# A recurrent decoder step: where the states of the sample sequences are loaded, summed and stored in the first tile

## The chip, the cores and the metric

The kernel runs on one core of a Trainium2 chip. The metric is device time in microseconds from start to end of one execution. The kernel before took 1485.17 us, the median of 3 runs (1482.73 to 1488.17).

## The reference, cut to what matters

One layer of a decoder is applied to a new sequence of 1024 tokens (the prompt) and, with the same weights, to one new token of each of 8 running sequences (the sample). Three groups of heads read one input projection and keep a recurrent state: GLA (6 heads, 32x64), DeltaNet (6 heads, 64x64) and HGRN2 (4 heads, 64x64). Then come an output projection, a mixture of 32 experts and a final norm.

```python
y_prompt, gla_p, dn_p, conv_p, hg_p = _trunk(x_prompt, z_gla, z_dn, z_conv, z_hg, *weights)
y_sample, gla_s, dn_s, conv_s, hg_s = _trunk(x_sample, state_gla, state_dn, state_conv, state_hgrn, *weights)
```

For a sample sequence the recurrence is a single step, here for DeltaNet (the other two have no correction of v):

```
S = exp(g) * S                        # decay of the state, (64 keys x 64 values) for each head
v = beta * (v - sum over keys k[key] * S[key, :])
S = S + k v^T                         # the new state: an output of the kernel
o = sum over keys q[key] * S[key, :]  # the output of the head
```

The states of all 8 sequences are inputs (`state_gla`, `state_dn`, `state_hgrn`) and, after the step, outputs of the same size: 0.375, 0.75 and 0.5 MB.

## The kernel before, in words

The prompt is cut into 8 tiles of 128 tokens (t = 0 to 7). For each tile TensorE computes the input projection in 17 units, one for each chunk of columns of w_in (mostly 1 MB); then follow the chunked recurrences, the output projection and the router. Behind the last tile come the experts (from 1087 us), which read their weights from HBM.

The engines have their own instruction streams, written out by hand, and wait for each other by semaphores: `done(eng, name, t)` waits until step `name` of tile t is over, `freed` until the tile before has given a buffer back. Nothing is reordered; an instruction that waits holds everything behind it on its engine.

**Weights.** SP issues the loads of the chunks, in the order of `stream`, into a ring of 4 buffers. `load_chunk(n)` waits until chunk n - 4 has been used. Chunks 0 to 16 are those of tile 0 (there TensorE runs the unit of the prompt, L1517 and L1521, and then that of the sample, L1534, whose semaphore `s_unit` frees the buffer), 17 to 33 those of tile 1, which TensorE computes while it works on tile 0's recurrence.

**The sample step.** The 8 x 16 sample states lie in `state_s`, one (sequence, head) in each partition: 48 rows of DeltaNet (`R_DN`), 48 of GLA, 32 of HGRN2; 4096 columns, key-major. SP loads them (L514 to L516) between chunks 11 and 12, when GpSimd has zeroed the space (`s_zero`). The 8 rows of projected values go to HBM by ScalarE's queue and come back to this layout by 16 small loads of SP (L536). VectorE then does the step in body(0), spread between its work for the prompt: `decay_s` (L1343, L1344), `read_keys_s` (L1347, the product with k), `correct_s` (L1350, the sum over keys), `update_s` (L1355, L1356 and the product with q, L1358; the step `s_state` is over behind L1356), `read_s` (L1361, the sum over keys; step `s_use`). The products are written to `tmp_s`, which is the space of E, zq and zk; so ScalarE's first exponentials of tile 0 (`decays(0)`, L897) wait for `s_use`.

**What lies on the states.** `state_s` shares its columns with vn, oc, x2, s_lin and s_dn of the prompt. Before these may be written the new states have to be in HBM. GpSimd stores them in body(0) behind its products for all four groups (L676 to L678), waits for the three stores, zeroes s_lin and s_dn (L680, L681; step `s_reset`), and goes on with the convolution of tile 1 (L590 to L604). ScalarE waits for `s_stored` in `load_x2` (L962), where it fetches the residual input into x2. That call stands in the loop over the levels, ahead of `norm_x(2)` (L754 to L760) and of the copy of level 5's product (L908), which TensorE needs for its next matmuls (L1479).

Of the kernel before, what the change touches and what calls it, by code (L numbers as in the profile page):

```python
# [6 lines left out]
ALU = mybir.AluOpType  # L7
ACT = mybir.ActivationFunctionType
AX = mybir.AxisListType.X
# [3 lines left out]
P = 128  # L13
# [66 lines left out]
NU = len(CHUNKS)  # L80
# [146 lines left out]
def trunk(nc, ctx, A, O, arena_cols, take, psum, bank, const, masks, x2_d, h2_d, lg, rows_d, so_d):  # L227
# [78 lines left out]
    st1, st2, st_s, gate_s, so, ng_s = take(4), take(4), take(4), take(64), take(64), take(64)  # L306
# [11 lines left out]
    def region(first, last):  # L318
        a, b = first.offset % 53200, last.offset % 53200 + last.shape[-1]
        return arena_cols(a, b)  # L320
# [17 lines left out]
    R_DN, R_GLA, R_HG = slice(0, 48), slice(48, 96), slice(96, 128)  # L338
# [7 lines left out]
    state_s = region(vn, s_spare)  # L346
    vec, ks_s = qs[:, 0:258], qs[0:48, 322:386]
# [14 lines left out]
    def step(name):  # L362
        name = once[name][0] if name in once else name
        if name not in sems:
            sems[name] = ctx.semaphore(name)
        return sems[name]

    def done(eng, name, t, n=1, per=1):

        eng.wait_ge(step(name), (once[name][1] if name in once else t * per) + n)  # L370
# [5 lines left out]
    def unit_at(t, k):  # L376

        return t * NU + (LAST_ORDER.index(k) if t == NT - 1 else k)
# [33 lines left out]
    n = 0  # L412
# [29 lines left out]
    def k_of(dt, rows=slice(0, P)):  # L442
        return qk2[rows, 4 + dt, :]
# [11 lines left out]
    with nc.Block() as block:  # L455
        @block.sync
        def _(sp):
            pb = lambda ap, n=P: ap.partition_broadcast(n)

            def load_chunk(n):  # L460
                kind, t, k = stream[n]
                if n >= RING:
                    was, wt, wk = stream[n - RING]
                    if was == "out":
                        sp.wait_ge(step("s_wo"), wk + 1) if wt == NT - 2 else sp.wait_ge(step("wo"), 4 * wt + wk + 1)
                    elif wt == 0:
                        sp.wait_ge(step("s_unit"), wk + 1)
                    else:
                        sp.wait_ge(step("unit_done"), unit_at(wt, wk) + 1)
                if kind == "in":  # L470
                    w, width = CHUNKS[k]
                    src = win_v[:, :, w:w + width]
                else:
                    width = WIDE
                    src = wout_v[:, :, WIDE * k:WIDE * k + WIDE]
                sp.dma_start(ring[n % RING][:, :, 0:width], src).then_inc(step(f"w_in{n % RING}"), 16)
# [32 lines left out]
            sp.dma_start(masks, A["shape_masks"]).then_inc(step("consts_in"), 16)  # L509
            for n in range(7, 12):  # L510
                load_chunk(n)
            sp.wait_ge(step("s_zero"), 2)
            sd_in = step("s_states_in")
            sp.dma_start(state_s[R_HG, :], A["state_hgrn"][0].rearrange("b h k e -> (b h) (k e)")).then_inc(sd_in, 16)  # L514
            sp.dma_start(state_s[R_GLA, 0:2048], A["state_gla"][0].rearrange("b h k e -> (b h) (k e)")).then_inc(sd_in, 16)
            sp.dma_start(state_s[R_DN, :], A["state_dn"][0].rearrange("b h k e -> (b h) (k e)")).then_inc(sd_in, 16)  # L516
            for n in range(12, NU + 5):
                load_chunk(n)


# [3 lines left out]
            q, k, dec, v_, o = 0, 64, 128, 192, ROW_AT  # L524
# [12 lines left out]
            sp.dma_start(O[8][0, :, 0:2, :], A["state_conv"][0, :, 1:3, :]).then_inc(st, 16)  # L537
            for n in range(NU + 5, NU + NU):
                load_chunk(n)
            done(sp, "s_out", 0)  # L540
            for n, (ap, h) in enumerate(((so[R_GLA, :], 6), (so[R_DN, :], 6), (so[R_HG, :], 4))):
                sp.dma_start(so_d[:, 384 * n:384 * n + 64 * h].rearrange("b (h e) -> b h e", e=DV), ap).then_inc(step("o_out"), 16)
# [32 lines left out]
        def _(pool):  # L575
# [34 lines left out]
            def body(t):  # L610
                n = t + 1
# [43 lines left out]
                for dt in range(4):  # L655
                    R = slice(0, DT_ROWS[dt])
# [4 lines left out]
                    e, k = E[dt % 2][R, :], k_of(dt, R)  # L661
# [9 lines left out]
                        ins = g.tensor_copy(el[R, dt:dt + 1], e[:, 1023:1024])  # L671
                    ins.then_inc(step("zks"), 1)
                if not t:
                    done(pool, "s_state", 0)
                    out_s = step("s_stored")
                    pool.dma_start(O[6][0].rearrange("b h k e -> (b h) (k e)"), state_s[R_GLA, 0:2048]).then_inc(out_s, 16)  # L676
                    pool.dma_start(O[7][0].rearrange("b h k e -> (b h) (k e)"), state_s[R_DN, :]).then_inc(out_s, 16)
                    pool.dma_start(O[9][0].rearrange("b h k e -> (b h) (k e)"), state_s[R_HG, :]).then_inc(out_s, 16)  # L678
                    pool.wait_ge(out_s, 48)
                    g.memset(s_lin, 0.0)  # L680
                    g.memset(s_dn, 0.0).then_inc(step("s_reset"), 1)  # L681
                if t < NT - 1:
# [8 lines left out]
            for t in range(NT):  # L691
                body(t)

        @block.scalar
        def _(act):
# [260 lines left out]
            def load_x2(t):  # L956
                if t:
                    act.wait_ge(step("x2_stored"), 16 * t)
                    done(act, "h2", t - 1)
                else:  # L960
                    act.wait_ge(step("s_stored"), 48)
                act.dma_start(x2, x_flat[t * P:t * P + P, :]).then_inc(step("x2_in"), 16)  # L962

            def store_x2(t):
# [120 lines left out]
        def _(dve):  # L1085
            v = nc.vector
            tt, ts, cp = v.tensor_tensor, v.tensor_scalar, v.tensor_copy
# [57 lines left out]
            def body(t):  # L1145
# [18 lines left out]
                if not t:  # L1164
                    read_keys_s()
                done(dve, "sqd", t)
                v.tensor_reduce(ssd, h3(ce[:, 0:768]), AX, ALU.add).then_inc(step("ssd"), 1)
                if not t:
                    correct_s()
# [39 lines left out]
                if not t:  # L1209
                    read_s()  # L1210
# [114 lines left out]
            def then(ins):  # L1325

                ins.then_inc(step("s_chain"), 1)
                n_chain[0] += 1
                dve.wait_ge(step("s_chain"), n_chain[0])


            s3, tmp3 = state_s.rearrange("p (k e) -> p k e", e=DV), tmp_s.rearrange("p (k e) -> p k e", e=DV)

            def over_v(ap):
                return ap.unsqueeze(2).to_broadcast([ap.shape[0], 64, DV])
# [4 lines left out]
            def decay_s():  # L1340
# [2 lines left out]
                then(cp(s_dec[R_DN, :], s_decay.to_broadcast([48, 64])))  # L1343
                then(tt(s3, s3, over_v(s_dec), ALU.mult))  # L1344

            def read_keys_s():
                then(tt(tmp3[R_DN], s3[R_DN], over_v(s_k[R_DN, :]), ALU.mult))  # L1347

            def correct_s():
                then(v.tensor_reduce(ks_s, tmp3[R_DN].rearrange("p k e -> p e k"), AX, ALU.add))  # L1350
                then(tt(s_val[R_DN, :], s_val[R_DN, :], ks_s, ALU.subtract))
                then(ts(s_val[R_DN, :], s_val[R_DN, :], s_beta, None, ALU.mult))

# [4 lines left out]
                then(tt(tmp3, s3, over_v(s_q), ALU.mult))  # L1358

            def read_s():  # L1360
                v.tensor_reduce(so, tmp3.rearrange("p k e -> p e k"), AX, ALU.add).then_inc(step("s_use"), 1)  # L1361
                done(dve, "s_use", 0)
                tt(so[R_HG, :], so[R_HG, :], gate_s[R_HG, :], ALU.mult).then_inc(step("s_pre"), 1)

# [1247 lines left out]
```

## Time and profile before

| | |
|---|---|
| median of 3 runs | 1485.17 us (1482.73 to 1488.17) |
| profiled execution | 1485.2 us, span of its trace 1483.4 us, mean granted clock 0.928 |
| TensorE (PE) | busy 1290.2 us, 87% of the span |
| VectorE (DVE), ScalarE (ACT), GpSimd (POOL) | 650.4, 408.9 and 470.2 us |
| DMA | 317 MB, mean 214 GB/s |
| chain that ended last | experts alone, from 1087 us |

The page gives shares over the whole span. Tile 0 with the input projection before it takes the first 231 us, and its slices differ from the later ones. So the first 231 us are read in the order of time, engine by engine, and the later tiles serve to show how long the same instructions take there. Times in the rows are us from the span's start; "idle before" is how long the engine had nothing to run, and the arrow names what ended it. PE is TensorE, DVE VectorE, ACT ScalarE, POOL GpSimd, SPq the queue on which SP issues DMAs.

### The profile page before, as it was taken

What the parts mean: (1) busy time and instruction counts of PE and PEld (TensorE: products, weight loads), DVE (VectorE), ACT (ScalarE), POOL (GpSimd) and SP (SyncE); (2) the same over time, 40 slices, a digit from 0 to 9 for tenths busy, and PEclk for the clock granted to TensorE, in tenths of its full rate; (3) what the DMA queues carried; (4) which work ended last, traced back from release to release, by engine and by line L of the source; (5) the groups of instructions that cost most, each with busy time, mean ns of one, the idle gap of its engine ahead of it and who ended that gap; (6) DMA issues with size and microseconds to landing.
All of it is one profiled execution on the core that took longest, in us unless ns stands there. A gap on an engine that the chain in (4) does not pass through costs nothing. (4 is left out here: it accounts for less than half of the span.)

```text
span 1483.4 us, 32235 instructions
## 1 busy us (share of the span) xinstructions
PE 1290.2 (87%) x13766; PEld 991.5 (67%) x13766; DVE 650.4 (44%) x1329; ACT 408.9 (28%) x856; POOL 470.2 (32%) x401
## 2 busy tenths in 40 slices
PE   7898879999999999999999989978745999986960
PEld 6688669879978978988987977767633333332320
DVE  2748735246245336335434625535353322221218
ACT  3134124225223323423422421422100112211113
POOL 1516263154235327236225416424001111111100
PEclk9999889999999999999999999988857999998985
DMA  9967345934833862773682563490078999999977
GB/s 272 253 199 221 103 145 169 280 110 154 274 118 121 257 198 96 236 238 102 200 271 90 161 214 98 130 141 21 7 260 284 363 320 379 374 361 368 367 289 312
DMA packets 273911, 317.28 MB, mean 214 GB/s; under 512 B 15196, under 2 KB 253352, under 8 KB 272336
## 3 DMA queue, kind: packets, MB, share of 16 engines
q1 hardware_dynamic: 261176, 275.81, 59.5%
q10 hardware_dynamic: 5792, 20.78, 4.1%
q0 software_dynamic: 6800, 18.62, 3.3%
q8 instruction: 110, 1.80, 0.5%
q14 instruction: 33, 0.27, 0.1%
HBM read 295.45 MB, written 27.01 MB: 217 GB/s over the span
## 5 line engine op out<-in xcount | busy, mean ns | idle before, releaser
L1521 PE MATMUL psum<-arena 128*128 128x256 f32 (+3 forms) x1536 | 312.8, 358 | 4.4 <-DMA arena<-in_w_in 4.4
L1521 PEld LDWEIGHTS psum<-arena 128*128 128x128 f32 x1536 | 258.7, 195 | 34.9 <-DMA arena<-in_w_in 4.6
L2366 PE MATMUL psum<-arena 128*64 128x512 f32 (+1 forms) x832 | 171.9, 630 | 21.2 <-DMA arena<-in_exp_w 21.2
L1232 DVE COPY_PREDICATED arena<-arena,psum 128x128 f32<-128x128 int32 x280 | 85.2, 304 | 142.6 <-PE psum L1710 135.7
L1517 PE MATMUL psum<-arena 128*128 128x128 f32 x1152 | 140.0, 282 | 4.3 <-DVE arena L1098 4.3
L1517 PEld LDWEIGHTS psum<-arena 128*128 128x128 f32 x1152 | 135.4, 197 | 6.9 <-issue 6.4
L662 POOL TENSOR_TENSOR arena<-arena 128x768 f32<-128x768 f32 (+1 forms) x32 | 59.1, 1846 | 246.6 <-ACT arena L897 246.6
L2366 PEld LDWEIGHTS psum<-arena 128*64 128x64 f32 (+1 forms) x832 | 53.8, 137 | 122.4 <-issue 120.5
L1479 PE MATMUL psum<-arena 64*64 64x64 f32 x3264 | 120.2, 227 | 14.1 <-ACT arena L908 10.3
L1479 PEld LDWEIGHTS psum<-arena 64*64 64x64 f32 x3264 | 108.2, 140 | 31.8 <-ACT arena L908 14.4
L1789 PE MATMUL psum<-arena 128*128 128x256 f32 x512 | 117.5, 389 | 0.8 <-ACT arena L973 0.8
L1789 PEld LDWEIGHTS psum<-arena 128*128 128x128 f32 x512 | 98.9, 196 | 14.7 <-ACT arena L973 1.2
L2208 POOL DMA_INDIRECT y_d<-arena x23 | 23.0, 1002 | 239.2 <-DVE arena L2307 218.4
L2313 DVE TENSOR_SCALAR arena<-psum 128x256 f32<-128x256 f32 x23 | 9.8, 425 | 170.1 <-PE psum L2366 170.1
L2385 PE MATMUL psum<-arena 128*64 128x512 f32 (+1 forms) x416 | 83.3, 594 | 0.7 <-DVE arena L2324 0.7
L740 ACT ACTIVATE arena<-psum 128x256 f32<-128x256 f32 (+2 forms) x72 | 25.1, 348 | 184.2 <-PE psum L1521 184.2
L1710 PE MATMUL psum<-arena 32*64 32x64 f32 (+1 forms) x2400 | 58.3, 230 | 13.0 <-DVE arena L1232 11.5
L604 POOL TENSOR_TENSOR arena<-arena 128x1152 f32<-128x1152 f32 x24 | 67.4, 2808 | 1.9
L2385 PEld LDWEIGHTS psum<-arena 128*64 128x64 f32 (+1 forms) x416 | 26.0, 131 | 54.2 <-issue 53.2
L2241 ACT ACTIVATE arena<-arena 128x256 f32<-128x256 f32 x23 | 9.6, 416 | 189.3 <-DVE arena L2313 189.3
L1710 PEld LDWEIGHTS psum<-arena 32*64 32x64 f32 (+1 forms) x2400 | 47.1, 137 | 19.5 <-DVE arena L1232 12.9
L626 POOL TENSOR_TENSOR arena<-arena 128x384 f32<-128x384 f32 x16 | 18.0, 1142 | 131.2 <-DVE arena L1136 131.2
(402 smaller groups left out, 1956.3 us busy)
## 6 DMA issues: line engine op xcount, KB each, us to landing
arena<-in_w_in SPq DMA_DIRECT2D x96, 1024.0 KB, 6.2
arena<-in_exp_w SPq DMA_DIRECT2D x96, 1024.0 KB, 13.1
arena<-in_w_out SPq DMA_DIRECT2D x32, 1024.0 KB, 5.8
arena<-in_w_in SPq DMA_DIRECT2D x24, 512.0 KB, 5.2
arena<-y_d SPq DMA_DIRECT2D x8, 1024.0 KB, 11.9
arena<-in_x_prompt ACTq DMA_DIRECT2D x15, 512.0 KB, 5.4
arena<-in_w_in SPq DMA_DIRECT2D x8, 576.0 KB, 4.7
arena<-in_w_in SPq DMA_DIRECT2D x8, 560.0 KB, 4.5
```

Source lines behind the costliest of these rows:

```text
L604: g.tensor_tensor(cv3, cv3, part, ALU.add).then_inc(step("tap" if i < 3 else "conv"), 1)
L662: g.tensor_tensor(near_z(zk[dt % 2][R, :]), near(e), near_qk(k), ALU.mult)
L740: ins = a(columns(w if w < QKV0 else w - CONV, n), src[:, 0:n], ACT.Copy)
L1232: ins = v.copy_predicated(h3(att_b)[:, h:h + 2, :], b3(q_mask[4 * half + j], 2, 64), new)
L1479: ins = mm(out[HALF[b], C], lhs(h, b), rhs(h, b), start=True, stop=True)
L1517: ins = mm(b[:, j * P:(j + 1) * P], w[:, c, j * P:(j + 1) * P], hT[:, c, :], start=(c == 0), stop=(c == KC - 1))
L1521: ins = mm(b[:, 0:n], hT[:, c, :], w[:, c, 0:n], start=(c == 0), stop=(c == KC - 1))
L1710: ins = mm(bank[6 + i][HALF[b], 64 * j:64 * j + 64], left[R, at:at + 64], right[R, at:at + 64], start=True, stop=True)
L1789: ins = mm(bank[6 if b else 3][:, WIDE * (m % 2):WIDE * (m % 2) + WIDE], oT[:, c * P:c * P + P], w[:, c, :], start=(c == 0), stop=(c == KC ...
L2208: pool.indirect_dma_start(y2_d, bass.IndirectOffsetOnAxis(ap=idx[q % NX][1], axis=0), Y[q % NX], None, bounds_check=2 * (NT * P + NS) - 1, ...
L2366: ins = mm(bank[2 + q % 2][at:at + width, :], xT[q % 2][:, c, at:at + width], w13[n % NB][:, c, :], start=(c == 0), stop=(c == KC - 1))
L2385: ins = mm(bank[4 + 2 * (q % 2) + b][at:at + width, :], hT[q % 2][:, c * P + at:c * P + at + width], w2[n % NB][:, c, 512 * b:512 * b + 51 ...
```

## The change

It has three parts. The loads of chunks 12 to 16 go ahead of the loads of the states on SP. Each of the two TENSOR_REDUCE over keys becomes six additions that halve the columns in place (`halve`), each waiting for the one before. The stores of the new states go from GpSimd's queue to SP's, behind tile 1's last chunk and a wait for `s_state`; GpSimd and ScalarE keep their wait for `s_stored`, and wait for `s_use` too, since the step may still read `state_s`.

```diff
             for n in range(7, 12):
                 load_chunk(n)
+            for n in range(12, NU):
+                load_chunk(n)
             sp.wait_ge(step("s_zero"), 2)
...
-            for n in range(12, NU + 5):
+            for n in range(NU, NU + 5):
                 load_chunk(n)
...
             for n in range(NU + 5, NU + NU):
                 load_chunk(n)
+            done(sp, "s_state", 0)
+            out_s = step("s_stored")
+            sp.dma_start(O[6][0].rearrange("b h k e -> (b h) (k e)"), state_s[R_GLA, 0:2048]).then_inc(out_s, 16)
+            sp.dma_start(O[7][0].rearrange("b h k e -> (b h) (k e)"), state_s[R_DN, :]).then_inc(out_s, 16)
+            sp.dma_start(O[9][0].rearrange("b h k e -> (b h) (k e)"), state_s[R_HG, :]).then_inc(out_s, 16)
             done(sp, "s_out", 0)
...
                 if not t:
-                    done(pool, "s_state", 0)
-                    out_s = step("s_stored")
-                    pool.dma_start(O[6][0].rearrange("b h k e -> (b h) (k e)"), state_s[R_GLA, 0:2048]).then_inc(out_s, 16)
...
-                    pool.wait_ge(out_s, 48)
+                    pool.wait_ge(step("s_stored"), 48)
+                    done(pool, "s_use", 0)
                     g.memset(s_lin, 0.0)
...
                     act.wait_ge(step("s_stored"), 48)
+                    done(act, "s_use", 0)
...
+            def halve(R, out):
+                n = 32
+                while n > 1:
+                    then(tt(tmp3[R, 0:n], tmp3[R, 0:n], tmp3[R, n:2 * n], ALU.add))
+                    n //= 2
+                return tt(out, tmp3[R, 0], tmp3[R, 1], ALU.add)
...
-                then(v.tensor_reduce(ks_s, tmp3[R_DN].rearrange("p k e -> p e k"), AX, ALU.add))
+                then(halve(R_DN, ks_s))
...
-                v.tensor_reduce(so, tmp3.rearrange("p k e -> p e k"), AX, ALU.add).then_inc(step("s_use"), 1)
+                halve(slice(0, P), so).then_inc(step("s_use"), 1)
```

On SP, from chunk 9 of the first tile on, the kernel before has the state loads between chunks 11 and 12:

```order
L476 DMA arena<-in_w_in 128x8x140 [waits s_unit]
L476 DMA arena<-in_w_in 128x8x256 [waits s_unit] x2
L514 DMA arena<-in_state_hgrn 32x4096 [waits s_zero]
L515 DMA arena<-in_state_gla 48x2048
L516 DMA arena<-in_state_dn 48x4096
L476 DMA arena<-in_w_in 128x8x256 [waits s_unit] x4
L476 DMA arena<-in_w_in 128x8x128 [waits s_unit]
L476 DMA arena<-in_w_in 128x8x256 [waits s_unit] x4
```

The changed kernel has them in the same place of SP's stream between chunk 16 (128 columns) and chunk 17:

```order
L476 DMA arena<-in_w_in 128x8x140 [waits s_unit]
L476 DMA arena<-in_w_in 128x8x256 [waits s_unit] x6
L476 DMA arena<-in_w_in 128x8x128 [waits s_unit]
L516 DMA arena<-in_state_hgrn 32x4096 [waits s_zero]
L517 DMA arena<-in_state_gla 48x2048
L518 DMA arena<-in_state_dn 48x4096
L476 DMA arena<-in_w_in 128x8x256 [waits s_unit] x4
```

Five chunks have gone ahead of the three states; the states stand in front of tile 1's first chunk now.

Further down SP's stream, behind tile 1's last chunk, the difference is this (`out` are the outputs in HBM, `so_d` the sample's head outputs; `once_dve` counts VectorE's steps of the sample):

```order
 L476 DMA arena<-in_w_in 128x8x256 [waits unit_done] x6
 L476 DMA arena<-in_w_in 128x8x128 [waits unit_done]
-L542 DMA so_d<-arena 8x6x64 [waits once_dve]
-L542 DMA so_d<-arena 8x6x64
-L542 DMA so_d<-arena 8x4x64
+L544 DMA out<-arena 48x2048 [waits once_dve]
+L545 DMA out<-arena 48x4096
+L546 DMA out<-arena 32x4096
+L549 DMA so_d<-arena 8x6x64 [waits once_dve]
+L549 DMA so_d<-arena 8x6x64
+L549 DMA so_d<-arena 8x4x64
```

The stores are new there, ahead of the sample's head outputs, which have only new line numbers.

On GpSimd, at the end of its products in tile 0, the kernel before has

```order
L671 COPY arena<-arena 128x1
L676 DMA out<-arena 48x2048 [waits once_dve]
L677 DMA out<-arena 48x4096
L678 DMA out<-arena 32x4096
L680 MEMSET arena 128x640 [waits s_stored]
L681 MEMSET arena 128x384
```

and the changed kernel has, in the same place,

```order
L678 COPY arena<-arena 128x1
L683 MEMSET arena 128x640 [waits once_dve,s_stored]
L684 MEMSET arena 128x384
L597 COPY arena<-arena 128x9x3 [waits unit_out]
L606 TENSOR_TENSOR arena<-arena 128x1152 [waits atd,cvT_mm,halo]
```

so that the memsets and the convolution behind them follow the products at once, if the stores have landed.

On VectorE, the sum over keys before (the row of 48x64 read 48x4096) and now:

```order
L1347 TENSOR_TENSOR arena<-arena 48x4096
L1167 TENSOR_REDUCE arena<-arena 128x12 [waits sqd,s_chain]
L1350 TENSOR_REDUCE arena<-arena 48x64
L1351 TENSOR_TENSOR arena<-arena 48x64 [waits s_chain]
L1352 TENSOR_SCALAR arena<-arena 48x64 [waits s_chain]
```

```order
L1171 TENSOR_REDUCE arena<-arena 128x12 [waits sqd,s_chain]
L1354 TENSOR_TENSOR arena<-arena 48x2048
L1354 TENSOR_TENSOR arena<-arena 48x1024 [waits s_chain]
L1354 TENSOR_TENSOR arena<-arena 48x512 [waits s_chain]
L1354 TENSOR_TENSOR arena<-arena 48x256 [waits s_chain]
L1354 TENSOR_TENSOR arena<-arena 48x128 [waits s_chain]
L1356 TENSOR_TENSOR arena<-arena 48x64 [waits s_chain]
L1363 TENSOR_TENSOR arena<-arena 48x64 [waits s_chain]
```

One instruction has become six; nothing else has changed its place on VectorE. The sum for the output is replaced in the same way, on 128 rows.

## Rows read from the trace of the kernel before

**Rows 1.** TensorE by stretch: us, busy us (count), granted clock, DMA share, GB/s.

```profile
231.00:886.00 655.00, 638.26 (x7132) 0.99 0.60 185
```

**Rows 2.** Waits of TensorE to 235 us: us in total, times, longest.

```profile
PE psum L1479 <- ACT arena L908: 10.3, 1, 10.3
...
PE psum L1646 <- ACT arena L897: 4.6, 1, 4.6
```

**Rows 3.** Timeline, SP's queue, weight chunks: start us, us, issue.

```profile
54.49 0.55 SPq L476 DMA_DIRECT2D arena<-in_w_in  x1
...
83.94 0.54 SPq L476 DMA_DIRECT2D arena<-in_w_in  x1
...
151.76 3.99 SPq L476 DMA_DIRECT2D arena<-in_w_in  x2
```

**Rows 4.** DMAs issued at 51.6, 54.5, 39.7 us: count, KB, us to landing.

```profile
arena<-in_state_dn SPq DMA_DIRECT2D x1, 768.0 KB, 18.4
...
arena<-in_w_in SPq DMA_DIRECT2D x1, 1024.0 KB, 18.1
...
arena<-in_w_in SPq DMA_DIRECT2D x1, 1024.0 KB, 6.5
```

**Rows 5.** Timeline of TensorE, 68 to 106 us: start, us, what [idle before].

```profile
72.67 5.53 PE L1521 MATMUL psum<-arena 128*128 128x256 f32 x16 [4.37 <-DMA arena<-in_w_in]
...
79.14 3.72 PE L1521 MATMUL psum<-arena 128*128 128x256 f32 x16
...
99.91 5.44 PE L1517 MATMUL psum<-arena 128*128 128x128 f32 x32 [2.82 <-DVE arena L1098]
```

**Rows 6.** Timeline of VectorE, tile 0: sample decay, both sums, two products.

```profile
118.78 4.43 DVE L1344 TENSOR_TENSOR arena<-arena 128x4096 f32<-128x4096 f32 x1
...
132.34 7.29 DVE L1350 TENSOR_REDUCE arena<-arena 48x64 f32<-48x4096 f32 x1
...
157.99 7.08 DVE L1361 TENSOR_REDUCE arena<-arena 128x64 f32<-128x4096 f32 x1
...
234.03 1.21 DVE L1288 TENSOR_TENSOR arena<-arena 128x1024 f32<-128x1024 f32 x1
235.27 0.96 DVE L1291 TENSOR_TENSOR arena<-arena 128x768 f32<-128x768 f32 x1
```

**Rows 7.** Timeline of GpSimd beside the key sum and, from 274.80, in tile 1.

```profile
132.13 0.86 POOL L642 TENSOR_TENSOR arena<-arena 128x384 f32<-128x384 f32 x1
136.83 1.55 POOL L646 TENSOR_TENSOR arena<-arena 128x768 f32<-128x768 f32 x1 [3.84 <-ACT arena L865]
...
274.80 1.54 POOL L646 TENSOR_TENSOR arena<-arena 128x768 f32<-128x768 f32 x1 [17.34 <-ACT arena L865]
276.30 2.26 POOL L647 TENSOR_TENSOR arena<-arena 128x768 f32<-128x768 f32 x1
```

**Rows 8.** Timeline of VectorE in tile 1, beside GpSimd's 274.80.

```profile
275.38 1.78 DVE L1171 TENSOR_TENSOR arena<-arena 128x768 f32<-128x768 f32 x1 [5.97 <-ACT arena L870]
```

**Rows 9.** Busy time by stretch, TensorE, after the wait of 4.6 us.

```profile
171.95:178.40 6.45, 6.45 (x68) 0.50 0.55 167
```

**Rows 10.** Timeline of GpSimd, then of ScalarE, at the end of the stores.

```profile
208.60 0.63 POOL L680 MEMSET arena<- 128x640 f32 x1 [8.41 <-DMA out<-arena]
...
208.98 1.06 ACT L754 ACTIVATE arena<-arena 128x1024 f32<-128x1024 f32 x1 [11.01 <-DMA out<-arena]
...
211.78 0.47 ACT L908 ACTIVATE arena<-psum 128x384 f32<-128x384 f32 x1
```

**Rows 11.** Timeline of TensorE: level 5 in tile 0, then in tile 1.

```profile
212.30 2.83 PE L1479 MATMUL psum<-arena 64*64 64x64 f32 x48 [10.27 <-ACT arena L908]
215.06 1.75 PE L1521 MATMUL psum<-arena 128*128 128x128 f32 x8
...
332.19 1.61 PE L1479 MATMUL psum<-arena 64*64 64x64 f32 x48
333.74 1.16 PE L1521 MATMUL psum<-arena 128*128 128x128 f32 x8
```

More of the change, by code:

```diff
@@ L673, in body @@
                 if not t:
-                    done(pool, "s_state", 0)
-                    out_s = step("s_stored")
-                    pool.dma_start(O[6][0].rearrange("b h k e -> (b h) (k e)"), state_s[R_GLA, 0:2048]).then_inc(out_s, 16)
-                    pool.dma_start(O[7][0].rearrange("b h k e -> (b h) (k e)"), state_s[R_DN, :]).then_inc(out_s, 16)
-                    pool.dma_start(O[9][0].rearrange("b h k e -> (b h) (k e)"), state_s[R_HG, :]).then_inc(out_s, 16)
-                    pool.wait_ge(out_s, 48)
+                    pool.wait_ge(step("s_stored"), 48)
+                    done(pool, "s_use", 0)
                     g.memset(s_lin, 0.0)
```

## The prediction

> **What bounds the kernel now.** I read the page first, for how the span divides: its chain of waits begins only at the experts, so it says nothing about the first tile, where every edit lies. The next view was busy time by stretch. From 231 to 886 us, tiles 1 to 5, TensorE is busy 638 of 655 us at a granted clock of 0.99 [rows 1]. It is the bound there, so a TensorE that leaves tile 0 earlier should carry the whole gain to the end. Third came who waited for whom before 235 us: besides the start, three waits stand out, 10.3 us for a ScalarE copy, 4.6 us for a ScalarE exponential and 4.4 us for a weight chunk [rows 2, 5]. Then I followed each in the order of time to what releases it.
>
> **The weight chunk.** SP issues the three sample-state loads and then chunk 12, at 54.49 us [rows 3]. That is the moment its ring buffer comes free (it waits for the sample matmuls of chunk 8), so the order on SP costs no issue time; the cost is in the transfer. Issued behind the states, the chunk lands after 18.1 us, at 72.6; the same 1 MB in the same stage, with no states in front, takes 6.5 [rows 4]. TensorE stood still for 4.37 us and ran its 16 matmuls in 5.53 us instead of 3.72 [rows 5], 1.8 us more than without a pause in front. After the change chunk 12 lands near 61 and the matmuls start at 68.3. Gain 4.4 + 1.8 = **6.2 us**. VectorE, ScalarE and the sample rows that follow are released by these matmuls and move with them; so do the 16 loads of rows back, which SP issues one after another before the sample step.
>
> What is late next? The states now go out after chunk 16, which waits for the sample matmuls of chunk 12, and ahead of chunk 17, the first of tile 1. Chunk 17 was issued at 83.94 [rows 3] and is now issued near 77.8. If it suffers as chunk 12 did, it lands at 77.8 + 18.1 = 95.9; TensorE needs it at 99.91 - 6.2 = 93.7 [rows 5]. So up to 2.2 us may be given back. I take 0, because chunk 16 ahead of the states is half the size of chunk 11, which is ahead of them now, and because chunk 17 is issued some 4 us behind the states as chunk 12 was, so that 18.1 is the upper end. The states themselves are first used by VectorE at 118.78 [rows 6], over 20 us after they land.
>
> **The halving.** The two TENSOR_REDUCE took 7.29 us (keys, 48 rows) and 7.08 us (reading, 128 rows) [rows 6]. Each becomes six additions over 2048, 1024, 512, 256, 128 and 64 elements. A TENSOR_TENSOR of this type takes 4.43 us for 4096 and 1.21 for 1024 elements [rows 6], thus 1.05 ns per element and 0.14 us fixed: 4032 elements and six fixed parts make 5.1 us, and six hops of 0.03 (the gap between the 1024 and the next instruction, which depends on it) 0.2: 5.3 us.
>
> For the reading sum nothing of GpSimd runs beside it: it saves 7.1 - 5.3 = **1.8 us**. This is on the path: ScalarE's exponential waits for it, and TensorE for the exponential (the 4.6 us).
>
> For the keys it is otherwise. A reduction left GpSimd alone: 7.29 us with, 7.08 without, while GpSimd's product at 136.83 took 1.55, the same as elsewhere [rows 6, 7]. An addition of two SBUF tiles does not: in tile 1 the product of 768 elements that began 0.6 us after GpSimd's took 1.78 us, where 0.96 is its length alone, and GpSimd's next one 2.26 instead of 1.54 [rows 6 to 8]. Each waited for the other's end, in turn. Under the key sum GpSimd has the end of one instruction (until 133.0) and then two of 1.5 us from 136.83 [rows 7]. The first addition is held 0.6 us, and two of the last short ones 1.5 each; a held addition has its 0.14 fixed part behind it. So 5.3 + 0.6 + 3.0 - 0.4 = 8.5 us: the key sum loses **1.2 us**. Unhindered it would gain 2.0; these are the two ends, and I take the loss because the rows of tile 1 are the same pair of instructions. VectorE's rows follow one another without idle time from the key sum to the end of the reading sum at 165.1 [rows 6], so both go straight through: net 0.6.
>
> The Trainium skill, "SBUF — State Buffer", section "Who interferes with whom", says the same as a rule: an instruction of VectorE with two SBUF inputs contends with one of GpSimd that reads SBUF, the second to issue being blocked to the end, and tensor_reduce never does. The trace agrees (1.78 against 0.96; 7.29 against 7.08). By this rule the sum below is 18.8; without it, it would be 22.0.
>
> The clock: after the 4.6 us the granted clock was 0.50 for 6.45 us [rows 9], of which half, 3.2 us, would be saved if it stayed up. TensorE's gap in front of it becomes about 3 us (4.6 less the 1.8 saved; the key sum moves both its ends). After the nearest gap, 2.82 us, the next matmuls still took 5.44 us [rows 5] for the work of 3.7 to 3.8. So I take 0, and keep 3.2 as an end.
>
> **The stores.** GpSimd issues them behind all its products of tile 0 and waits 8.41 us for them [rows 10]. ScalarE may not load the residual input into that space earlier: it idles 11.01 us, then norms the x of tile 2, and only after that copies the level's product at 211.78 [rows 10] on which TensorE waits 10.27 us [rows 11]. Now SP issues them behind the load of tile 1's last chunk. That load was issued by 155.8 [rows 3]; the states are final by 158, since the reading sum that starts there needs them [rows 6]. With the 8.4 us and their issue they have landed by some 168 us, 30 us ahead of ScalarE, which is ready at 208.98 - 11.01 = 198.0. From its release at 208.60 it took 0.4 us to the norm and 2.8 more to the copy [rows 10]; from 198.0 that is 201.2. TensorE's own work ends at 212.30 - 10.27 = 202.03, so it goes on there, with the copy done: 10.2 us. And without the pause the next two groups should take 1.61 and 1.16 us, as in the same place of tile 1, not 2.83 and 1.75 [rows 11]: 1.8 more. Sum **12.0 us**. On GpSimd the memsets of s_lin and s_dn and the convolution of tile 1, which stood behind the wait, come forward by the same 10 us, so they meet the same instructions of VectorE as now. Behind the stores on SP wait only the sample outputs and the chunks of tile 2, needed from 231 us on. The ends of this term are 0, where the stores still hold ScalarE, and 12.0; the 30 us of room decide for the second. The added waits for s_use are over at 165 us.
>
> **Sum.** 6.2 - 1.2 + 1.8 + 12.0 = 18.8 us. The profiled execution took 1485.2 us, which is the median of the runs to 0.03 us; its span is 1483.4, so 1.8 us lie around it and stay. 1485.2 - 18.8 = **1466.4 us**.
>
> **Rivals.** (A) The halving is not hindered and the clock stays up: 3.2 and 3.2 us more, 1460. For it: the two engines may fall into another rhythm, half a microsecond decides; against it: tile 1's rows. (B) The states hold tile 1's first weights: 2.2 us, and, if the clock falls once more as at 72.67, another 1.8: 1468.6 to 1470.4. For it: 18.1 us; against it: chunk 16 is half as long. (C) The stores do not leave the path, because SP gets to them late or they are slow beside weights, and 10 to 12 us stay: about 1478. Against it: 30 us of room. (D) Nothing arrives at the end, since a later stage takes it back: within 4 us of before. Against it: TensorE is full in tiles 1 to 5. (E) Slower: without its pauses TensorE is granted less clock in tiles 1 to 5, the place where 638 us of matmul stand. Each hundredth of clock costs 6.4 us there, so from a mean of 0.96 on the gain is eaten, and at 0.95 the time is 1466.4 + 26 = 1492. Against it: 0.99 over 655 us without pauses.
>
> **How the numbers follow.** The forecast 0.58, A 0.15, B 0.14, C 0.05, D 0.04, E 0.04. What can be told from no change is 0.3%, 4.5 us. A, B, C and the forecast are all faster by more: 0.92; D is the same, 0.04; E slower, 0.04. The range takes in A and B and the 2 to 3 us by which runs of this kernel differ: 1458.5 to 1474.5.
>
> **What would show it.** Right, if chunk 12's wait near 68 us is gone and chunk 17 has none; if the reading sum's six additions last 5.3 us, and the key sum's 8 to 9 with two of the short ones at 1.5 us or more; if ScalarE loads the residual near 191 us and TensorE has no wait over 1 us before that level. Wrong, if a new wait for a weight chunk stands near 94 us, if the key sum lasts under 6 us, if the stores are still in flight at ScalarE's load, or if the clock from tile 1 to 5 is under 0.97.

## The result and the profile after

The changed kernel takes 1462.82 us (median, 1459.85 to 1464.87), the kernel before 1485.72 on the same chip; the ratio is 0.9865 with a 95% interval of 0.9846 to 0.9885, so 17 to 23 us less. Forecast: 1466.4. The profiled execution after has a span of 1458.0 us, 25.4 less than before; it is among the fastest of its runs, so some 3 us of these 25.4 are no part of the median.

Where the time went is read between two instructions that both traces have: unit 6 of tile 0's projection (at 42.41 us before and 40.62 after; units have the numbers of their chunks) and the first unit of tile 2's projection, which TensorE computes beside tile 1's recurrence (230.61 and 208.32). Ahead of unit 6 nothing was changed, and the same code reaches it between 39.8 and 44.2 us in the traces of this study, so a start counted from the span's beginning would mix that in. The stretch takes 188.20 us before and 167.70 after: 20.5 us less. Line numbers after are up to 12 higher: L1521 is L1533, L1517 is L1529, L1479 is L1491.

TensorE's waits to 235 us after (total, times, longest; answers to [rows 2]). The 10.3 us for ScalarE's copy and the 4.4 for a weight chunk are gone. What came up is the last line, an "issue", a stand for which the profile shows no releaser:

```profile
PE psum L1614 <- DVE arena L1159: 4.4, 1, 4.4
...
PE psum L1658 <- ACT arena L900: 2.9, 1, 2.9
PE psum L1533 <- issue: 2.7, 1, 2.7
```

The timeline of TensorE (start us, us, what, idle before) answers to [rows 5]. Unit 12 no longer waits, 3.72 us instead of 4.37 + 5.53. Unit 16, the last of tile 0, halts after two of its 16 matmuls (the expectations below call it unit 15), and the first unit of tile 1, needing chunk 17, waits for VectorE alone:

```profile
65.18 3.72 PE L1533 MATMUL psum<-arena 128*128 128x256 f32 x16
...
83.82 0.49 PE L1533 MATMUL psum<-arena 128*128 128x128 f32 x2
87.05 1.72 PE L1533 MATMUL psum<-arena 128*128 128x128 f32 x14 [2.74 <-issue]
...
92.84 3.81 PE L1529 MATMUL psum<-arena 128*128 128x128 f32 x32 [2.16 <-DVE arena L1102]
```

Of the DMAs issued at 72.8 and 74.6 us (KB, us to landing; compare [rows 4]) the states' largest lands after 12.7 us and chunk 17 behind it after 13.8, at 88.4, well ahead of 92.84. But in the view of the DMA queues for 84 to 85 us there is a packet of the queue that loads instructions, the only one between 71 and 90 us:

```profile
arena<-in_state_dn SPq DMA_DIRECT2D x1, 768.0 KB, 12.7
```
```profile
arena<-in_w_in SPq DMA_DIRECT2D x1, 1024.0 KB, 13.8
```
```profile
q8 instruction: 1, 0.02, 6.9%
```

VectorE's two sums after (compare [rows 6]): the key sum's six additions take 8.25 us, from 123.82 to 132.07, and the reading sum's 5.32:

```profile
123.82 8.00 DVE L1354 TENSOR_TENSOR arena<-arena 48x2048 f32<-48x2048 f32 x5
131.85 0.22 DVE L1356 TENSOR_TENSOR arena<-arena 48x64 f32<-48x64 f32 x1
...
150.36 5.06 DVE L1354 TENSOR_TENSOR arena<-arena 128x2048 f32<-128x2048 f32 x5
155.45 0.23 DVE L1356 TENSOR_TENSOR arena<-arena 128x64 f32<-128x64 f32 x1
```

GpSimd's two products beside the key sum stand in it from 128.41 to 131.67 (answers to [rows 7]). Of the six additions the first took 2.79 us, the fourth 1.65 and the fifth 1.52, where e9, with nothing of GpSimd beside them, has 2.27, 0.42 and 0.28:

```profile
128.41 1.58 POOL L653 TENSOR_TENSOR arena<-arena 128x768 f32<-128x768 f32 x1 [3.94 <-ACT arena L868]
129.95 1.72 POOL L654 TENSOR_TENSOR arena<-arena 128x768 f32<-128x768 f32 x1
```

SP issues the stores at 148.17 us, and they land after 6.2 to 8.8; ScalarE loads the residual at 187.20 without a wait, norms, and has the copy for level 5 done at 191.77 (answers to [rows 10]). TensorE goes through level 5 at tile 1's pace (answers to [rows 11]):

```profile
148.17 0.65 SPq L544 DMA_DIRECT2D out<-arena  x1
148.87 0.42 SPq L545 DMA_DIRECT2D out<-arena  x1
149.33 0.92 SPq L546 DMA_DIRECT2D out<-arena  x1
```
```profile
187.20 0.36 ACTq L966 DMA_DIRECT2D arena<-in_x_prompt  x1
187.62 1.06 ACT L757 ACTIVATE arena<-arena 128x1024 f32<-128x1024 f32 x1
...
191.28 0.49 ACT L911 ACTIVATE arena<-psum 128x384 f32<-128x384 f32 x1 [0.77 <-PE psum L1491]
```
```profile
191.82 1.61 PE L1491 MATMUL psum<-arena 64*64 64x64 f32 x48
193.37 1.16 PE L1533 MATMUL psum<-arena 128*128 128x128 f32 x8
...
208.32 3.74 PE L1529 MATMUL psum<-arena 128*128 128x128 f32 x32
```

In tiles 1 to 5, the same 655 us counted from the end of the stretch (busy time by stretch: us, busy us and count, granted clock, DMA share, GB/s), TensorE is as full as before and at the same clock [rows 1]. So it hands the gain on to the end. The second row is a piece behind the wait for the exponential, 6.17 us at a clock of 0.64; the same matmuls took 7.10 us before (171.95 to 179.05, at 0.52), of which [rows 9] has the first 6.45:

```profile
208.69:863.69 655.00, 637.73 (x7128) 0.99 0.60 185
162.55:168.72 6.17, 6.17 (x93) 0.64 0.58 173
```

### The profile page after: what moved, and what is told of

Its sections match the earlier page's. It is cut to its first block and busy times, and to the rows that moved or that the text cites. A ratio compares the mean times of both kernels' runs of the same rounds, so it can differ in the third digit from the quotient of the medians.

```text
span 1458.0 us, 32247 instructions
## 1 busy us (share of the span) xinstructions
PE 1278.5 (88%) x13766; PEld 982.5 (67%) x13766; DVE 648.4 (44%) x1339; ACT 409.0 (28%) x856; POOL 470.0 (32%) x398
## 5 line engine op out<-in xcount | busy, mean ns | idle before, releaser
L1533 PE MATMUL psum<-arena 128*128 128x256 f32 (+3 forms) x1536 | 310.2, 356 | 2.7 <-issue 2.7
L1533 PEld LDWEIGHTS psum<-arena 128*128 128x128 f32 x1536 | 257.4, 194 | 32.8 <-issue 3.4
L1529 PE MATMUL psum<-arena 128*128 128x128 f32 x1152 | 137.6, 279 | 3.6 <-DVE arena L1102 3.6
L1529 PEld LDWEIGHTS psum<-arena 128*128 128x128 f32 x1152 | 133.1, 195 | 6.2 <-issue 5.8
L1491 PE MATMUL psum<-arena 64*64 64x64 f32 x3264 | 115.9, 222 | 4.6 <-issue 2.0
L1491 PEld LDWEIGHTS psum<-arena 64*64 64x64 f32 x3264 | 104.0, 136 | 21.5 <-issue 14.1
L1722 PE MATMUL psum<-arena 32*64 32x64 f32 (+1 forms) x2400 | 58.0, 228 | 13.5 <-DVE arena L1236 12.1
## 6 DMA issues: line engine op xcount, KB each, us to landing
arena<-y_d SPq DMA_DIRECT2D x8, 1024.0 KB, 11.9
```

The source lines that it names most:

```text
L1491: ins = mm(out[HALF[b], C], lhs(h, b), rhs(h, b), start=True, stop=True)
L1529: ins = mm(b[:, j * P:(j + 1) * P], w[:, c, j * P:(j + 1) * P], hT[:, c, :], start=(c == 0), stop=(c == KC - 1))
L1533: ins = mm(b[:, 0:n], hT[:, c, :], w[:, c, 0:n], start=(c == 0), stop=(c == KC - 1))
L1722: ins = mm(bank[6 + i][HALF[b], 64 * j:64 * j + 64], left[R, at:at + 64], right[R, at:at + 64], start=True, stop=True)
```

## The experiments

Each run was timed against the kernel before on its chip. "Stretch" is the time from unit 6 to tile 2's first unit in the run's one trace, against 188.20 before. It leaves out the start and the later stages, which differ by some us between runs of the same code, so it tells small parts apart better than the times do.

| run | time | ratio to before (95%) | stretch |
|---|---|---|---|
| changed kernel | 1462.82 | 0.9865 (0.9846 to 0.9885) | -20.5 |
| e1 loads alone | 1480.4 | 0.998 (0.9963 to 0.9997) | -3.3 |
| e2 stores alone | 1469.31 | 0.9904 (0.9883 to 0.9924) | -12.1 |
| e3 halving alone | 1482.12 | 0.9995 (0.9974 to 1.0017) | 0.0 |
| e4 key sum a reduction | 1465.09 | 0.9872 (0.9849 to 0.9895) | -18.4 |
| e5 both reductions | 1465.2 | 0.9879 (0.9857 to 0.99) | -19.9 |
| e6 gates later | 1465.38 | 0.9881 (0.986 to 0.9902) | -16.5 |
| e7 key sum alone | 1475.13 (once) | - | -18.3 |
| e8 stores on GpSimd's queue | 1466.1 | 0.9881 (0.9861 to 0.9901) | -17.4 |
| e9 states two chunks later | 1468.31 | 0.9904 (0.9888 to 0.9921) | -16.7 |
| e10 states spread | 1462.99 | 0.9864 (0.9847 to 0.988) | -21.4 |
| e11 states in quarters | 1465.39 | 0.9887 (0.987 to 0.9903) | -18.6 |
| e12 spread, key sum reduced | 1460.55 | 0.985 (0.9823 to 0.9876) | -20.9 |

**One part alone.** e1 and e2 make only their part of the change, e3 both halvings:

```diff
-            for n in range(7, 12):        # e1: states behind chunk 16
+            for n in range(7, NU):
-                    pool.dma_start(O[6]...  # e2: three stores and their wait
+            sp.dma_start(O[6]...            #     behind tile 1's chunks
-                v.tensor_reduce(so, ...)    # e3: and the key sum likewise
+                halve(slice(0, P), so)
```

> The kernel before with one part of the change: chunks 12 to 16 go ahead of the state loads; both sums and the stores as before. Theory 1 (the prologue's gain is the pause of 4.4 us at chunk 12 and the slow clock that follows a pause): 6 to 9 us less than before, no wait for chunk 12 or 17, the first unit of tile 1 at about 3.8 us instead of 5.4, and the waits of 4.6 and 10.3 us still there. Theory 2 (the gain beyond 4.4 us comes from stalls without a releaser that fell elsewhere by chance): about 4.4 us less, and the first unit of tile 1 at 5.4 us again.

> The kernel before with one part of the change: the stores from SP's queue; state loads and both sums as before. Theory 1 (ScalarE's wait for the stores held TensorE): 12 us less than before (10.2 of wait, 1.8 of clock), the waits of 4.4 and 4.6 us still there. Rival (a later wait takes its place, since the convolution of tile 1 now meets other work): less than 8 us.

> The kernel before with one part of the change: both sums by halving. Theory 1 (key sum 8.3 us against 7.3, because GpSimd holds its additions; reading sum 5.3 against 7.1): 0.8 us less than before, up to 4 if the clock stays up behind TensorE's shorter pause; not to be told from no change by the times, so read from the trace. Rival (the additions are as long as their count says, 5.3 each, and VectorE's chain gains 3.6): 3.6 us less, TensorE's wait for the exponential at 1 to 1.6 us.

e2 came out as forecast: 12.1 us in the stretch (14.2 by the times, the interval reaching down to 11.3), and the other waits as before. From the level's second matmuls behind the exponential to tile 2's first unit, every kernel with the stores moved takes the same 11.9 us less: 10.1 of wait and 1.8 of slower matmuls behind it. e1 brought only half of its forecast, 3.3 in the stretch and 3.0 by the times. Its chunk wait is gone and tile 1's first unit takes 3.81 us, as theory 1 has it, but TensorE halts in unit 16, longer than in the changed kernel, and runs slower behind it (2.33 us for what took 1.72, at a granted clock of 0.70 instead of 1.00):

```profile
87.31 2.33 PE L1521 MATMUL psum<-arena 128*128 128x128 f32 x14 [3.00 <-issue]
94.03 3.81 PE L1517 MATMUL psum<-arena 128*128 128x128 f32 x32 [1.76 <-issue]
...
205.33 2.82 PE L1479 MATMUL psum<-arena 64*64 64x64 f32 x48 [10.54 <-ACT arena L908]
```

To unit 16 e1 gains 7.5 us (43.20 instead of 50.72); the halt gives back 1.8 by the end of tile 1's first unit; a short operation of VectorE behind the key sum, held by GpSimd (1.24 instead of 0.29), costs about 1.2 with what follows; and behind the wait for the stores, which is still there, the matmuls are 1.9 slower than before; 0.6 comes back between these two. e3 brought nothing although its sums gained (the key sum took 5.28 us, not the 8.3 of theory 1): from the end of tile 1's first unit to the product after the exponential it took 60.29 us instead of 60.96, and the matmuls behind that 1.3 us less, but then came the stores. GpSimd issued them 1.6 us earlier, counted from unit 6, yet the last took 10.50 us to land instead of 8.88, so ScalarE was released no earlier (in e1, where it took 9.14, 5.2 us earlier). Why it took longer in e3 stays open. The wait on level 5 grew to 11.9:

```profile
210.13 2.82 PE L1487 MATMUL psum<-arena 64*64 64x64 f32 x48 [11.90 <-ACT arena L908]
```

**The halving and GpSimd.** e4 and e5 put one or both reductions back into the changed kernel; e6 (key sum reduced) and e7 (halved) move GpSimd's three gate products behind its product kd in tile 0, in e7 with a wait that keeps kd's neighbours behind the key sum too; in e8 GpSimd issues the stores, ahead of its later products.

```diff
-                then(halve(R_DN, ks_s))                       # e4 to e6
+                then(v.tensor_reduce(ks_s, tmp3[R_DN]..., AX, ALU.add))
-                g.tensor_tensor(gc[:, 0:768], ...)            # e6, e7: three products,
+                if not t:                                     # behind kd
+                    gates()
+                if not t:                                     # e7, ahead of GpSimd's
+                    done(pool, "qkn", t)                      # products of the key sum
+                if not t:                                     # e8, behind kd
+                    pool.dma_start(O[6]...
```

> The changed kernel with the key sum by TENSOR_REDUCE again and the reading sum by halving. Theory 1: the key sum takes 7.3 us and the key product's end is unchanged, so VectorE's chain and TensorE behind it are 0.9 to 1.0 us earlier than in the changed kernel, TensorE's wait for kb falls from 1.4 to about 0.5 us. Rival (halving is the faster form for both): the time grows by 1 us or more.

> The changed kernel with both sums by TENSOR_REDUCE: loads and stores moved, no halving. Theory 1: 0.8 us more than the changed kernel (key sum 0.95 better, reading sum 1.8 worse), by the trace; TensorE's wait for the exponential about 4.6 us. Rival (halving carried 3.6 us): 3.6 us more.

> The changed kernel with the key sum by TENSOR_REDUCE, and, in tile 0, GpSimd's three products for the output gates behind its product for kd, where it is idle, instead of beside the key product. Theory 1 (GpSimd's reads hold VectorE's products of two tiles): the key product takes 4.4 us instead of 6.0, the key sum 7.3; TensorE's wait for the exponential falls from 2.9 us to near 0.5 and the time by 2.4 to 3 us below the changed kernel, unless the gate products now hold the state update instead, which lasts 14.4 us in the changed kernel. Rival (no contention; the 48-row product is slow by itself): the key product stays at 6.0.

> The changed kernel, both sums by halving, with nothing of GpSimd beside the key sum: in tile 0 its gate products go behind kd, and its two products with the decay wait for the end of the key correction. Theory 1: the six additions of the key sum take 5.3 us together instead of 8.25. Rival (short additions on 48 rows are slow by themselves): they stay at 8.

> The changed kernel with the three stores back on GpSimd's queue, but issued as soon as the states are final, behind kd, without a wait there. Theory 1 (the moment of the stores matters, not the queue): the same time as the changed kernel within 1 us, ScalarE's load of the residual unhindered. Rival (GpSimd's queue is slow in itself or is held by VectorE's work): the stores land later, and up to 12 us come back.

The times cannot tell these apart: e4, e5, e6 and e8 lie within 1 us of each other, and e6 is not the 2.4 to 3 us below the changed kernel that theory 1 gave it. The traces can. The plainest is e5, whose halt and whose path to the end of tile 1's first unit are those of the changed kernel: from there to the product behind the exponential it takes 0.9 us longer, and its stretch is 0.6 longer, faster matmuls behind that product making the difference. So both halvings together are worth 0.6 to 0.9 us, where theory 1 had 0.8 and its rival 3.6. With GpSimd out of its way, in e7, the key sum takes 5.27 us. That settles the price of the additions; the 8.25 of the changed kernel hold 2.98 us of waiting. But the time does not stay gained. GpSimd's products come later and meet the next additions and products of VectorE, of which the first takes 5.77 instead of 5.05 and five of the reading sum's additions 6.70 instead of 5.06. Timeline of VectorE in e7:

```profile
128.19 5.02 DVE L1362 TENSOR_TENSOR arena<-arena 48x2048 f32<-48x2048 f32 x5
133.24 0.22 DVE L1364 TENSOR_TENSOR arena<-arena 48x64 f32<-48x64 f32 x1
...
135.72 5.77 DVE L1375 TENSOR_TENSOR arena<-arena 128x4096 f32<-128x4096 f32 x1
...
153.91 6.70 DVE L1362 TENSOR_TENSOR arena<-arena 128x2048 f32<-128x2048 f32 x5
```

e6 shows the same: the key product took 4.41 instead of 5.99 with the gates away, and the product for the reading 5.92 instead of 4.43; what the key product gained went into a wait of VectorE of 1.92 us for ScalarE. So the measure is from the key sum's start to the reading sum's end, on VectorE without a pause: 32.7 us before, 31.9 in the changed kernel, 31.4 in e3, 31.2 in e4, 32.9 in e5, 33.4 in e6 and 32.7 in e7. The reading sum's gain stands: 5.3 for 7.1 wherever GpSimd is not beside it, and the wait for the exponential is 2.87 us in e4 and 4.64 in e5. Halving the keys is worth nothing or costs half a microsecond; e4, which leaves it out, is within 2.3 us of the changed kernel in the time and 2.1 worse in the stretch, where its halt in unit 16 and the slower matmuls behind it cost 2.0 more and slower matmuls behind the exponential 0.9, against 0.8 gained at the key sum and ahead of it. e6 and e7, built to free it, are worse. In e8 the stores land 6.3 to 10.5 us after their issue, ScalarE is not held and level 5 has no wait, as with the stores on SP: what matters is that the stores no longer stand behind GpSimd's products, not which queue carries them. (Its stretch is 3.1 us longer than the changed kernel's, not within 1 us as expected: 1.7 are lost ahead of the end of tile 1's first unit, 1.4 behind the exponential, none at the stores.) Of e7's one time nothing is read: its stretch is like that of the others, and the rest lies in later stages.

**The halt in unit 16.** It is in all seven kernels that load the states behind chunk 16 (2.6 to 3.3 us) and in none of those that load them earlier, which halt near 66 us instead (0.65 to 1.01). The last four runs ask whether it belongs to the place in the program or to the states in flight.

```diff
-            for n in range(12, NU):             # e9: states two chunks later
+            for n in range(12, NU + 2):
+            for n in range(12, 14): ...         # e10: gla here
+            for n in range(14, 15): ...         #      hgrn here
+            for n in range(15, NU): ...         #      dn here
+                for c in range(0, dst.shape[1], 1024):   # e11: ten loads
+                    sp.dma_start(dst[:, c:c + 1024], src[:, c:c + 1024])
```

> The changed kernel with the three state loads two weight chunks later on SP's queue: behind chunk 18 instead of behind chunk 16, so they go out near 80 us instead of 70.6. In the changed kernel TensorE stands still for 2.74 us at 84.3 to 87.05 in the third matmul of unit 15, with no releaser, and a 16 KB packet of its instruction queue lands at 84.5 to 85.0, as the last of the states does. Theory P (the instruction packet waits behind the states' transfers): the packet lands some us earlier than the stall, unit 15 runs with no pause over 1 us, and a shorter or equal pause may come up some 10 us later; tile 0 ends 1 to 3 us earlier counted from unit 11, time 1460 to 1464. Theory Q (the pause belongs to that place of the program, whatever is in flight): the pause of 2.6 to 3.3 us stays at unit 15's third matmul, time as the changed kernel, 1462 to 1466. Either way chunk 19, now directly behind the states, lands near 98 and is needed at 100.7, so it costs nothing or up to 2 us.

> The changed kernel with the three state loads one by one between the weight chunks: gla (384 KB) behind chunk 13, hgrn (512 KB) behind chunk 14, dn (768 KB) behind chunk 16. Theory P (the instruction packet waits behind the states' bytes in flight): only dn is in flight at 80 to 85 us, less than half of the bytes, so the pause at unit 15 falls from 2.7 to 3.3 us to about 1.3 or less; chunks 14 and 15 land 2 to 4 us later than now and still before they are needed (issued some 9 us ahead, landing in 6.5), so no wait comes in their place. Time 1461 to 1465. Theory Q (the pause belongs to its place in the program): 2.6 to 3.3 us at unit 15 as now.

> The changed kernel with the same state loads at the same place, each cut into pieces of 1024 columns: ten loads with rows of 4 KB instead of three with rows of 16 and 8 KB. The same bytes at the same time, smaller packets. If it is the length of the single packets that holds the instruction packet (theory P1), the pause at unit 15 falls below 1.5 us; if it is the bytes in front of it (theory P2) or the place in the program (theory Q), it stays at 2.6 to 3.3 us. Seven more issues of 0.4 us on SP put chunk 17 some 3 us later, needed at 92.8: it lands near 91. Time 1461 to 1466.

> The changed kernel with four state loads, one at a time between the weight chunks (gla behind chunk 12, hgrn behind 13, half of dn's columns behind 14, the other half behind 16), and the key sum as one reduction again, the reading sum halved. Theory P (the instruction packets wait behind the states' bytes in flight): with 384 KB of states in flight at 75 to 85 us the pause at unit 15 is under 0.5 us, and no weight chunk is waited for, each landing within 10 us where some 14 lie between issue and use. Key sum 7.3 us, reading sum 5.3, from the key sum's start to the reading sum's end 31.3 us as with the key reduced before. Against the changed kernel 2.7 us for the pause and 0.5 for the key sum: 1459 to 1464. If instead the pause at unit 15 stays, 1462 to 1466; if a chunk is now waited for near 70 to 80 us, 1464 to 1470.

| us from the span's start | instruction packet | unit 16's third matmul due | halt |
|---|---|---|---|
| changed kernel | 84.5 to 85.0 | 84.3 | 2.74 |
| e1 | 84.5 to 85.0 | 84.3 | 3.00 |
| e11 quarters | 84.75 to 85.0 | 85.1 | 2.50 |
| e10 spread | 86.25 to 86.5 | 87.8 | 1.12 |
| e12 four pieces | 81.0 to 81.25 | 83.6 | none |
| e9 later | 79.5 to 79.75 | 84.5 | none |

(The packet is placed by the view of the DMA queues in windows of 0.25 or 0.5 us; due is unit 16's start and the 0.49 us of its first two matmuls.) The halt ends 2.1 to 2.8 us behind the packet in each, and where the packet comes 2.4 us or more ahead of need there is none. The packet's place follows the states: it is early where they are spread or out later. In the kernel before, the packet landed at 64 to 65 us, again while the states were in flight, and TensorE halted for 0.91 at 66.3. So theory P holds and Q falls: the program sets where a halt can fall, the transfers in flight whether it does. The places are the same in every trace. Counted over TensorE's instruction records, the halts near 66 us, in unit 16 and, smaller, twice in later tiles come 1024, 1791, 6911 and 9727 records behind one near 38 us, which all fourteen traces have (0.6 to 3.1 us). To within one record these are multiples of 256, and the queue brings 110 packets for 28,076 records, one for every 255; that ties the packets to TensorE. Other "issue" gaps, as the 1.76 in e1's second row above, do not fall on such places. That the packet waits in its own queue for the states' transfers is inferred from these landings; the trace doesn't show the waiting, and the halt near 38 us stands ahead of any state load, so other transfers may do the same. Cutting the rows to a quarter changed nothing (e11), so it is not the length of the single rows. The Trainium skill, "DMA: Bandwidth & Descriptors", section "Queues, rings and completion order", says that a DMA engine serves its queues in turn and drains a whole packet, a group of descriptors, before it switches. Whether a shorter row makes a shorter packet in that sense no run here shows, so e11 neither bears this out nor speaks against it. Rows of TensorE in e10, e11 and, where unit 16 runs through, e12:

```profile
88.94 1.72 PE L1537 MATMUL psum<-arena 128*128 128x128 f32 x14 [1.12 <-issue]
```
```profile
87.59 3.12 PE L1535 MATMUL psum<-arena 128*128 128x128 f32 x14 [2.50 <-issue]
```
```profile
83.12 2.24 PE L1540 MATMUL psum<-arena 128*128 128x128 f32 x16
...
89.81 5.44 PE L1536 MATMUL psum<-arena 128*128 128x128 f32 x32 [2.54 <-DVE arena L1109]
```

The last row shows why removing the halt is worth less than its length. With the halt, TensorE's next gap is 2.16 us and tile 1's first unit takes 3.81 at a granted clock of 1.00; without it the gap is 2.54 (2.82 in e9 and before) and the unit takes 5.44, at a mean of 0.69. From unit 16's start to that unit's end it is 12.8 us in the changed kernel, 12.1 in e12, 12.2 in e9 and before, 11.2 in e10, but 14.0 in e1, 14.1 in e11 and 14.8 in e4, where the clock fell behind the halt (0.70, 0.51 and 0.51 in the rest of unit 16). e9 pays elsewhere: SP takes 13.76 us to issue the rows back instead of 11.29, VectorE begins the sample step 2.4 us later, counted from unit 6, and a product behind it takes 2.84 us instead of 1.56, so TensorE waits 8.94 us for VectorE instead of 4.38 and the time misses the 1460 to 1464 us of theory P:

```profile
120.89 2.18 PE L1614 MATMUL psum<-arena 128*128 128x128 f32 x9 [8.94 <-DVE arena L1159]
```

In e12 there is no halt in unit 16 and no wait for a chunk, though chunks land after up to 14.0 us instead of the expected 10, and from the key sum's start to the reading sum's end it takes 31.3 us, as expected. It is the fastest kernel of the study, 1460.55 us, and e10 stands at 1462.99; their intervals overlap with the changed kernel's, so neither is shown to be faster than it.

## Why the prediction came out

By its own terms, each from the two traces between unit 6 and tile 2's first unit:

| term | predicted | measured |
|---|---|---|
| weight chunk | -6.2 | -7.5 to unit 16, +0.6 to the end of tile 1's first unit, +0.2 to the key sum |
| key sum | +1.2 | +0.9 |
| reading sum | -1.8 | -1.8 |
| clock after the exponential | 0 | -0.9 |
| stores | -12.0 | -10.1 wait, -1.8 slower matmuls |
| sum | -18.8 | -20.5 (from unrounded terms) |

The stores and the reading sum were right to 0.1 us, mechanism and size. The key sum was right for this trace (8.25 us, forecast 8.5: GpSimd's two products are waited for, in turn, and the additions held are those that were named), but its 0.9 is one draw of several: the same additions took 8.25 us in e10 and e11 too, but 5.27 in e3 and e9 and 5.40 in e8, and what was spared there was mostly waited for by the instructions behind them. Over the traces, from the key sum's start to the reading sum's start, it is 26.0 to 26.5 us in the six kernels that halve (e7 left out) and 25.7 to 26.6 in the six that reduce (e6 left out): 0.3 us worse on average, within their spread. 1.2 was too much.

The weight chunk is the term that was incomplete. Its 6.2 us are there (4.37 + 1.81), and 1.3 more, 0.9 of them the halt near 66 us, which I had not read as belonging to the states. "What is late next" was asked of chunk 17 only, and chunk 17 was not late. Late was TensorE's own instruction packet. Rival B had the right culprit, the states in flight, and the wrong victim. In the profiled run this cost 0.6 us; in e1 1.8 and in e4 2.6, so the 20 us of the ratio, not the 25 of the two profiled executions, are what a run may expect.

Behind the exponential the clock was a little higher (0.64 for 0.52 over the same matmuls), 0.9 of the 3.2 us that I had kept as an end and of the 1.7 by which the stretch beat the sum. That was luck, since the shorter wait does not go with it in the other traces: from the product behind the exponential to the level's second matmuls it took 12.74 us before and 11.80 after, but 11.47 in e2 and 11.37 in e5, which have the old wait of 4.6, and 12.73 in e4 and 13.23 in e8, which have the new one of 2.9. Rivals A, C, D and E fell: the additions were held, the stores landed by 158.1 us, 29 ahead of ScalarE, and tiles 1 to 5 kept 0.99.

Taken one by one the parts give 3.3 + 12.1 + 0.0 in the stretch, 5 us less than together. Of these 3.8 lie at and behind the wait for the stores, which ends tile 0's chain on ScalarE: while it is there, what is gained ahead of it went partly into a longer wait (10.27, 10.54, 11.90) and a slower restart. The rest is the net of the halts, the holds and the clock ahead of it, which differ from trace to trace.

## What to carry to other kernels

Work on the gain that ends a stage's chain first: a gain ahead of a wait that another engine ends can be lost in it, as the halving's was in e3's trace. When a block of transfers is moved, ask not only which data comes late but whether an engine's instructions are loaded in the same window; an "issue" halt at the same instruction in every run, with a packet of the instruction queue landing shortly before it ends, is the sign. Where two engines hold each other, measure from before the contended stretch to the next joint event, since a hold that is avoided in one instruction tends to come back in the next.

## What was not expected of the hardware

- TensorE halted for 1.1 to 3.3 us in unit 16 where a packet of the instruction queue came late; the halt ended 2.1 to 2.8 us behind it (84.5 to 85.0, on again at 87.05). That the one causes the other is inferred from the times in the table.
- Of two gaps of nearly the same length, the one of 2.16 us left the next 32 matmuls at 3.81 us, behind those of 2.54 and 2.82 us they took 5.44. The length of the gap alone does not decide: behind halts of 2.74 and 2.76 us (changed kernel, e5) the granted clock was 1.00, behind one of 2.50 (e11) 0.51.
- A tensor_reduce over 4096 strided elements took 7.1 to 7.3 us, 1.7 ns per element, while six additions of the same tile took 5.3 in all.
